# A 128x128 product of the unit matrix with itself ahead of every half level of the delta rule's triangular solve

## The reference

```python
kb = k * beta[..., None]
lower = jnp.where(strict, jnp.einsum('nbhid,nbhjd->nbhij', kb, k) * decay, 0.0)
a = lower + jnp.eye(CHUNK, dtype=f32)
u = lax.linalg.triangular_solve(a, v * beta[..., None], left_side=True, lower=True, unit_diagonal=True)
w = lax.linalg.triangular_solve(a, kb * jnp.exp(gc)[..., None], left_side=True, lower=True, unit_diagonal=True)
attn = jnp.einsum('nbhid,nbhjd->nbhij', q, k) * decay
def step(S, inp):                       # then a scan over the chunks, in each direction
    w_i, u_i, qg_i, a_i, kd_i, gl_i = inp
    v_new = u_i - jnp.einsum('bhck,bhkv->bhcv', w_i, S)
    o = jnp.einsum('bhck,bhkv->bhcv', qg_i, S) + jnp.einsum('bhij,bhjv->bhiv', a_i, v_new)
    S = S * jnp.exp(gl_i)[..., None, None] + jnp.einsum('bhck,bhcv->bhkv', kd_i, v_new)
    return S, o
```

## Time and profile before

| | |
|---|---|
| median of 3 runs | 1846.41 us (1844.94 to 1851.91) |
| the profiled execution's own time | 1849.15 us |
| its span in the trace | 1847.4 us |
| granted TensorE clock, mean over the span | 0.911 of full speed |
| PE busy | 1685.9 us, 91% of the span |
| stretch of the delta rule, layer 0 | about 380 to 590 us from the span's start |
| stretch of the delta rule, layer 1 | about 1267 to 1480 us |
| granted clock in the stretch 383.00 to 588.40 | 0.67 |

### The profile page before, as it was taken

How to read it: one execution, slowest core, us unless ns; L and a number is a source line. 1 busy time by engine, 2 the same in 40 slices (tenths; PEclk the granted TensorE clock), 3 DMA queues, 4 the chain that set the end, 5 groups by cost and what they waited for, 6 DMA issues and landing times. The chain is left out here.

```text
span 1847.4 us, 49314 instructions
## 1 busy us (share of the span) xinstructions
PE 1685.9 (91%) x21858; PEld 1367.8 (74%) x21858; DVE 972.8 (53%) x1471; ACT 613.4 (33%) x1300; POOL 856.7 (46%) x822
## 2 busy tenths in 40 slices
PE   4999999968877899999999999997878889999998
PEld 2888999957666755555879999996777775555586
DVE  2663336444442587779337413554444357777921
ACT  4311220132332444456234132013222244454611
POOL 1001395054442387885320139705444238788532
PEclk9899999976677999999999999997676599999999
DMA  9345112210000000113320210221000000011322
GB/s 334 135 160 197 37 59 69 77 45 16 10 5 4 22 6 21 31 31 136 118 96 27 60 59 26 82 92 48 16 10 4 4 23 6 17 33 32 120 91 91
DMA packets 69810, 112.93 MB, mean 61 GB/s; under 512 B 9824, under 2 KB 41824, under 8 KB 69600
## 3 DMA queue, kind: packets, MB, share of 16 engines
q1 hardware_dynamic: 69136, 109.62, 17.7%
q10 hardware_dynamic: 464, 0.17, 0.1%
HBM read 90.30 MB, written 19.47 MB: 59 GB/s over the span
## 5 line engine op out<-in xcount | busy, mean ns | idle before, releaser
L1738 POOL TENSOR_TENSOR attn_accp<-attn_accp,attn_pr 128x1024 f32<-128x1024 f32 x110 | 269.5, 2450 | 42.9 <-ACT attn_pr L1804 37.2
L95 PE MATMUL ps<-in_h_hi,in_w_hi 128*128 128x384 f32 x720 | 244.1, 339 | 2.5 <-DVE in_h_lo L616 2.5
L97 PE MATMUL ps<-in_h_hi,in_w_lo 128*128 128x384 f32 x720 | 242.4, 337 | 0.0
L2008 DVE TENSOR_REDUCE attn_ql<-ps 128x1 f32<-128x1152 f32 x128 | 172.5, 1355 | 102.0 <-PE ps L1926 101.6
L1804 ACT ACTIVATE attn_pr<-ps 128x512 f32<-128x512 f32 x292 | 158.7, 595 | 170.5 <-PE ps L1970 161.7
L1969 PEld LDWEIGHTS ps<-attn_QH,attn_KH 128*128 128x128 f32 x292 | 55.4, 190 | 122.0 <-ACT attn_pr L1804 55.2
L95 PEld LDWEIGHTS ps<-in_h_hi,in_w_hi 128*128 128x128 f32 x720 | 135.7, 188 | 9.3 <-issue 7.5
L1979 PE MATMUL ps<-attn_pr,z 128*64 128x512 f32 x520 | 139.5, 615 | 0.0
L97 PEld LDWEIGHTS ps<-in_h_hi,in_w_lo 128*128 128x128 f32 x720 | 135.5, 188 | 0.0
L1497 DVE TENSOR_TENSOR delta_TR<-delta_TR,ps 128x128 f32<-128x128 f32 x180 | 49.3, 274 | 161.2 <-PE ps L1220 130.6
L1969 PE MATMUL ps<-attn_QH,attn_KH 128*128 128x512 f32 x292 | 131.3, 450 | 0.0
(11 more groups left out here) (313 smaller groups left out, 3934.3 us busy)
## 6 DMA issues: line engine op xcount, KB each, us to landing
in_w<-in_w_in SPq DMA_DIRECT2D x21, 1024.0 KB, 5.5
z<-in_w_mod SPq DMA_DIRECT2D x8, 2048.0 KB, 8.1
gates<-in_gate SPq DMA_DIRECT2D x48, 192.0 KB, 1.9
attn_gt<-gates SPq DMA_DIRECT2D x34, 256.0 KB, 2.6
z<-in_x_sample SPq DMA_DIRECT2D x16, 512.0 KB, 6.3
zz<-in_w_mod SPq DMA_DIRECT2D x4, 2048.0 KB, 13.3
out_w<-in_w_out SPq DMA_DIRECT2D x16, 512.0 KB, 6.2
out_y<-z SPq DMA_DIRECT2D x16, 512.0 KB, 2.9
```

Source lines behind the costliest of these rows:

```text
L95: nc.tensor.matmul(out, a_hi(i), b_hi(i), start=(i == 0), stop=False)
L97: last = nc.tensor.matmul(out, a_lo(i), b_hi(i), start=False, stop=(i == n - 1))
L1738: nc.gpsimd.tensor_tensor(acc, a, pr[:, n % 4], ALU.add).then_inc(pool_added, 1)
L2008: nc.vector.tensor_reduce(ql[:, a % 4, blk, HD:HD + 1], ps[:, bank:bank + 3, 0:GRP], AX_XY, ALU.max).then_inc(mx_read, 1)
```

## The change

Ahead of every half level (phases `x1` to `x5` and `y1` to `y5`) PE also multiplies the unit matrix by itself once, into columns 256 to 383 of PSUM bank 0 (`x`) or bank 2 (`y`), which nothing reads. It does so in the turns 1 to 8, not in turn 0. The product has no wait of its own and stands ahead of the phase's waits. That makes 10 products in each of 8 turns in each of 2 layers, 160 in all; as float32 products each is two weight loads and two matmuls on PE.

```diff
@@ -1253,8 +1253,14 @@
                                                     skip_group_check=True)
                     return last
 
+                def keep_busy(bank):
+
+                    nc.tensor.matmul(ps[:, bank, 256:384], m["ident"], m["ident"], start=True, stop=True)
+
                 def phase(j, name):
                     t, jj = turn_tile(j), j % 2
+                    if name[0] in "xy" and j:
+                        keep_busy(0 if name[0] == "x" else 2)
                     if name == "kq":
                         if j >= 1:
                             pe.wait_ge(ea_out, 2 * j)
```

## The result

| | before | changed |
|---|---|---|
| median of 4 runs on one chip | 1846.01 us | 1900.58 us (1898.52 to 1907.46) |
| ratio, 95% interval | | 1.0295 (1.0261 to 1.0330) |
| the profiled execution's own time | 1849.15 us | 1907.46 us |
| its span | 1847.4 us | 1905.7 us |

The median rose by 54.6 us; +16 was forecast, and 1900.6 lies above the range's end of 1889.

The account below looks back on a forecast made before the run. PE was taken to set the pace, by its half clock and its code's arrival. Per turn 2.5 + 0.6 - 1.9 = 1.2 us, sixteen turns +19, less 3: +16 us, 1862 us against the median; stated range 1842 to 1889.

Parts of the forecast that it names:

- my 3.8: Delta-rule turns: a packet of PE's code every 3.8 us, so a floor of 22.7 us under the 23.7 us turn.
- Term 1: Five early squares in the gapless half-clock stretch of a turn lengthen it by 0.5 us each, 2.5 us a turn.
- my lower bound: Price of a square on PE at half clock: 0.44 us, from 0.22 us for this shape at full clock.
- my pricing by passes: A square on PE priced as two passes like the 128x128 transposes, 0.26 us each at half clock, 0.53 us.
- by that rule I had 0.61: A square paying a 0.17 us tiling-mode switch on PE costs 0.61 us; the sum would be 10 us higher.
- Term 2: Five late squares hide in PE's stops at 0 us; the code of all ten costs 0.6 us a turn, 9.6 us.
- the two stops: PE stands still 1.28 and 1.81 us within groups of a turn's quick part, 3.1 us to cover late squares.
- Term 3: Squares raise the delta rule's clock from 0.65 to about 0.78, which gives back 1.9 us a turn.
- its limit: A turn can gain no more from the clock than the code packets allow: 22.7 + 0.6 = 23.3 us.
- The 3 us taken off: Work after each layer's last turn (`uw` and `au` of turn 8) may meet full clock: -3 us in all.
- the clock unmoved: Rival: delta-rule clock stays, so terms 1 and 2 stand, +40 to +50 us, 1886 to 1896 us; chance 0.14.

Follow-up runs that it names:

- e1: Changed kernel with each added 128x128 product made a 32x32 product of 16 columns, same number of instructions: 1856.52 us, 1.0077 of the kernel before.
- e8: Kernel before, without squares, with the four transposes (phase kq) moved ahead of y1, right behind uw0: 1851.77 us, 1.0031 of the kernel before.
- e9: Kernel before, without squares, leaving out the second chunk's products in x4 and y4 (part of the result missing): 1815.76 us, 0.9828 of the kernel before.
- e12: The changed kernel once more, unaltered, on the same chip as e11: 1900.74 us, 1.0297 of the kernel before.
- e5: Changed kernel with all ten squares of a turn in one row ahead of x1: 1890.04 us, 1.0228 of the kernel before.
- e6: Changed kernel with two squares in each of the ten places, 320 in all: 1889.32 us, 1.0208 of the kernel before.
- e2: Changed kernel whose added products keep the 128x128 weights but take 16 columns in place of 128: 1894.11 us, 1.0284 of the kernel before.
- e3: Changed kernel with squares only ahead of y3, x4, y4, x5 and y5, 80 of 160: 1859.55 us, 1.0088 of the kernel before.
- e10: Changed kernel with two squares each ahead of x1, y1, x2, y2 and x3 and none later: 1886.15 us, 1.0220 of the kernel before.
- e7: Changed kernel whose added products have the neighbours' 32x32 shape but still 128 columns: 1878.53 us, 1.0174 of the kernel before.
- e4: Changed kernel with squares only ahead of x1, y1, x2, y2 and x3, 80 of 160: 1883.83 us, 1.0234 of the kernel before.
- e11: Changed kernel with all ten squares, leaving out the second chunk's products in x4 and y4: 1880.68 us, 1.0186 of the kernel before.

## Why the prediction was wrong

The step that failed is that PE's own work was never put beside the code as a second limit. Ten squares make a turn at the half clock one of 28.1 us, over the code's 24.0; I took them for work that costs 2.5 us, is half hidden, and is partly paid back by a rising clock. The clock's missing gift, 1.9 us a turn, is the largest part of the missing 2.3; the price of a square and the cover for the late ones are the rest.

**What held.** PE set the pace, partly by its clock and partly by its code, and the code was a floor close under the pace: e1 and layer 0 of e8 (clock different, time the same) and e9 (instructions out, -32 us) show it. The cost sat in the delta rules, the projection kept its length, q8 brought 176 packets, and stops lay 3.5 to 3.9 us apart (e12, e5). By 3.91 us a packet, taken from the seven turns, the code's floor is the pace itself; my 3.8 had it 1.0 us below.

The Trainium skill (Runtime: NRT & Kernel Launch, Instruction fetch mechanics) calls the crossing between blocks mostly hidden. e9 disagrees: nine packets fewer are worth 32 us.

**Term 1, the price of a square: too small.** I took 0.5 us at half clock from the four transposes. It is 0.72 us at half and 0.42 at full. The columns cost what my lower bound said (0.44; the second of a pair 0.43, and 0.22 at full). What the estimate left half out is the price of standing alone among other shapes, 0.29 us, paid by each square (e6). Four transposes in a row share it. Taking columns away would not have helped much (e2), since the loads are then no longer hidden, which my pricing by passes could not show. Five early squares hold 3.5 us a turn and add 3.3 (the one behind the transposes adds 0.42), not 2.5.

The Trainium skill (TensorEngine Tiling (Array Packing), Tiling Modes, Key Properties) has that passing to another mode drains the engine. The trace agrees that a lone square costs 0.29 us more than the second of a pair, but doesn't tell a drain from a load that is no longer hidden; by that rule I had 0.61, still too little.

**Term 2, the late squares at 0 us: wrong.** They cost 1.0 us a turn by e3's ratio, 0.3 of it code; e3's one trace shows the code alone. "It runs while PE would be waiting" took the two stops, 3.1 us, for a store that any work nearby may draw on. As e3 shows, a stop gives nothing to work that stands behind it. And it is there only when PE is quick; when the clock stays at half there is no stop, and a late square ahead of y3, x4 or y4 costs its full 0.72 like an early one. The squares ahead of x5 and y5 do fill time that PE spends anyway, 0.8 us of the 1.46 that the two hold, but inside the groups of x5 and y5 and not in the stops that I had named.

**Term 3, the clock, -1.9 us a turn: didn't come.** 0.60 in place of the 0.78 put down. A single square is not "the kind of work that precedes the rise": squares one at a time leave the clock near where it was, pairs and piles raise it (e5 0.69, e6 0.79 and 0.85, e10 0.76 and 0.70), and a 16-column product or one on a small tile holds it at 0.50 for a whole layer (e2, e7), below before's 0.66. Even where it rose the time did not fall, which the prediction did say of its limit. The 3 us taken off for the work behind the last turns didn't come either: from the eighth `au` to the ninth there are 12.31 and 10.62 us, where before had 11.04 and 10.54.

**How the terms were put together.** I added PE time and code time and took the clock's gift off. The runs fit another rule better: a turn takes about the time of its code, or, where it stays at the half clock, PE's time if that is longer. Per turn, in us:

| | PE wholly at half clock | code, at 3.91 us a packet | measured |
|---|---|---|---|
| before | 22.0 | 23.4 | 23.46, 23.29 |
| changed | 28.1 | 24.0 | 27.25, 26.41; e12 26.06, 26.97 |
| e1 | 22.7 | 24.0 | 23.67, 23.89 |
| e2 | 26.4 | 24.0 | 26.28, 26.23 |
| e3 | 24.8 | 23.7 | 23.69, 23.63 |
| e4 | 25.3 | 23.7 | 25.53, 25.47 |
| e5 | 26.6 | 24.0 | 25.87, 26.27 |
| e9 | 22.0 | 21.4 | 21.61, 22.08 |

The PE column is the 22.0 with the prices of the added products (in e1 0.09 us each, none ahead of x5 and y5). The before row is where 3.91 comes from; the others are tests. In the change 1.4 us of the squares fit into the gap from 22.0 to 23.4, and 4.7 show where a turn stays at half clock, about 0.6 (the code) where it rises. 3.46 on average lies between. e4 and e5 are the weak rows. e4 stands slightly above both columns though its clock is over 0.50, and e5 stays near the PE column at a clock of 0.69: there the squares crowd one part of the turn, and the other keeps its stops. e6 and e10, whose clocks are 0.70 to 0.85, have 24.7 to 27.0 us, also above the code's 24.6 and 24.0. So the rule seems to go packet by packet and not by the turn; that it does was not measured apart.

Had the forecast asked how long a turn would be wholly at the half clock (12.55 us of it stood in the earlier trace rows, and the same trace has the other groups at that clock in other places), the squares would have been seen to turn a bound by code into one by PE. The rival that fits is the second, the clock unmoved, at 1886 to 1896; it was given 0.14, and it too was 5 us low, for which it had named the reason, the price of the squares' switches.

**Open.** What in a pair or a pile raises the clock and in a single square doesn't was not separated. Nor was what a lone square pays for, the change of shape or a load that nothing hides. Why packets come 3.9 us apart isn't shown either. No kernel here that computes everything was faster than the one before; e8 was the try. Whether the code's share could be won by fewer instructions with the same result was not tried.

## What to carry to other kernels

Before work is added to an engine that seems to have idle time, compute both limits of the stretch, its time at the slow clock without gaps and the time its code takes to arrive, and see which one the new work moves. An instruction of another tile shape set alone among small ones costs much more than its columns: here 0.72 us where a second one beside it costs 0.43. Where stops came at even distances inside a group of equal instructions, fewer instructions helped (e9) and a higher clock did not (e8, layer 0). Products that run side by side hide this, since they are code without being time.

## What was not expected of the hardware

- A 16-column float32 product with 128x128 weights costs 0.54 us at half clock and one of 128 columns 0.72 (e2).
- At the half clock 32 matmuls of 32x32 on half of the array take 0.97 us, and 64 on both halves 0.99 (e11): leaving the other half's out saves code alone.
- The second load of a lone product's 128x128 weights runs under its first columns: the two loads take 0.50 us both in a square of 0.72 and in a narrow product of 0.54 (PEld's rows of the change and of e2).
- With PE busy for 183 of 184 us, on small tiles with narrow full-array products among them, the granted clock stayed at 0.50, 1.2 GHz (e2).
- The granted clock of one stage differs between executions of one kernel: 0.55 and 0.63 in layer 0 of the change, 0.63 and 0.57 in layer 1.
